# Mixture-of-experts layers on one core: each expert's combination placed ahead of the next expert's weights and gate/up product

## The reference, cut to what matters

```python
g = argmax(x @ w_group)                      # a token's group, of 4
vals, loc = top_k(elog_of_group, 2)          # two of the group's 8 experts
gates = pg * softmax(vals)
hb = silu(xb @ w_gate[e]) * (xb @ w_up[e])   # 1024 -> 512, per expert e
y[token] += gates * (hb @ w_down[e])         # 512 -> 1024
```

## Time and profile before

| | us |
|---|---|
| median of 3 runs | 1930.45 |
| lowest and highest | 1920.70, 1933.29 |
| the profiled execution, device time | 1928.58 |
| its span | 1926.7 |

### The profile page before, as it was taken

One profiled execution on the slowest core, in us unless ns is written; L12 is line 12 of the kernel. 1 busy time (PEld: TensorE's weight loads), 2 busy tenths in 40 slices (PEclk: granted clock), 3 DMA queues, 4 the chain that ended last, 5 costly groups with the idle time before them and its releaser, 6 DMA issues. The chain is left out here.

```text
span 1926.7 us, 28099 instructions
## 1 busy us (share of the span) xinstructions
PE 1617.7 (84%) x12625; PEld 1025.5 (53%) x12625; DVE 523.0 (27%) x1257; ACT 231.7 (12%) x519; POOL 75.7 (4%) x97
## 2 busy tenths in 40 slices
PE   7999768878776999957557565899999999999998
PEld 5654435444444875523233232686886446588643
DVE  5752233433134114214211111621210022521002
ACT  2311011101100001100200000120110003211000
POOL 2000100000000000000000000330000000000000
PEclk9999889988887998978787887999999999999999
DMA  9357999999998844999999999734444334143410
GB/s 343 122 231 285 377 426 424 424 424 425 426 424 343 332 193 188 421 419 410 423 407 410 426 410 425 277 138 175 169 155 151 127 113 177 42 175 133 173 44 22
DMA packets 88054, 540.04 MB, mean 280 GB/s; under 512 B 7326, under 2 KB 9438, under 8 KB 54140
## 3 DMA queue, kind: packets, MB, share of 16 engines
q1 hardware_dynamic: 86044, 531.24, 68.6%
q0 software_dynamic: 1888, 6.95, 1.0%
HBM read 531.89 MB, written 6.29 MB: 279 GB/s over the span
## 5 line engine op out<-in xcount | busy, mean ns | idle before, releaser
L725 PE MATMUL ps<-ring,work 128*32 128x256 f32 x3968 | 302.4, 467 | 223.0 <-DMA ring<-in_moe_w_up 221.5
L725 PEld LDWEIGHTS ps<-ring,work 128*32 128x32 f32 x3968 | 157.4, 130 | 355.7 <-issue 303.7
L702 PE MATMUL ps<-ring,work 128*128 128x512 f32 x768 | 331.0, 592 | 0.0
L676 PE MATMUL ps<-hT,ring 128*128 128x256 f32 (+2 forms) x1488 | 330.0, 384 | 0.0
L676 PEld LDWEIGHTS ps<-hT,ring 128*128 128x128 f32 x1488 | 283.2, 191 | 45.4 <-issue 3.3
L702 PEld LDWEIGHTS ps<-ring,work 128*128 128x128 f32 x768 | 145.7, 190 | 182.2 <-issue 181.3
L738 PE MATMUL ps<-ring,multi 128*32 128x256 f32 x1984 | 121.5, 386 | 13.7 <-ACT multi L1467 11.7
L2033 DVE TENSOR_TENSOR rowb<-rowb,ps 128x128 f32<-128x128 f32 x64 | 18.4, 288 | 386.9 <-ACT rowb L1462 386.9
L2039 DVE COPY multi<-ps 128x256 f32<-128x256 f32 x64 | 27.2, 425 | 264.7 <-PE ps L738 264.5
L738 PEld LDWEIGHTS ps<-ring,multi 128*32 128x32 f32 x1984 | 58.9, 110 | 73.8 <-issue 21.8
L1462 ACT ACTIVATE rowb<-ps 128x128 f32<-128x128 f32 x64 | 17.8, 278 | 562.4 <-PE ps L725 562.4
(11 more groups left out here) (452 smaller groups left out, 1310.8 us busy)
## 6 DMA issues: line engine op xcount, KB each, us to landing
ring<-in_moe_w_gate SPq DMA_DIRECT2D x62, 2048.0 KB, 18.8
ring<-in_moe_w_up SPq DMA_DIRECT2D x62, 2048.0 KB, 23.3
ring<-in_moe_w_down SPq DMA_DIRECT2D x62, 2048.0 KB, 22.3
ring<-in_w_ff SPq DMA_DIRECT2D x32, 2048.0 KB, 8.2
ring<-in_sc_w_in SPq DMA_DIRECT2D x6, 2048.0 KB, 17.8
ring<-in_lru_w_in SPq DMA_DIRECT2D x4, 2048.0 KB, 15.4
ring<-in_ssm_w_glu SPq DMA_DIRECT2D x4, 2048.0 KB, 18.7
ring<-in_lru_w_out SPq DMA_DIRECT2D x2, 2048.0 KB, 20.2
```

The source lines that it names most:

```text
L676: mm = pe.matmul(ps[:, bank, 0:n], w[:, k, P * c:P * c + P], hT[:, k, t0:t0 + n], start=(k == 0), stop=(k == DC - 1))
L702: mm = pe.matmul(ps[0:m, 2 + 2 * b + hf, :], left[:, kk, t0:t0 + m], w[:, k, 512 * hf:512 * hf + 512], start=(kk == 0), stop=(kk == 4 * la ...
L725: mm = pe.matmul(ps[32 * q:32 * q + 32, bank, 0:256].rearrange("p (u n) -> p u n", u=2), x[:, k, :], gu[:, k, :, 2 * P * (q // 2):2 * P * ...
```

## The change

The wait for and the issue of `weigh_in(e - 1)`, with the waits and the register load of e = 1, move from behind `gate_up` of e to a place ahead of the wait for the weights of e. Nothing is added or removed.

```diff
                     pe.wait_ge(*nth(f"xT_ready{l}", 2 * g + (1 if e == 0 else 2)))
+                    if e == 1:
+                        pe.wait_ge(*nth(f"spread_out{l}", 1))
+                        pe.wait_ge(*nth(f"rounds_known{l}", 1))
+                        rounds = pe.value_load(rounds_i[0:1, l:l + 1], min_val=1, max_val=MAX_ROUNDS)
+                    if e >= 1:
+                        weigh_in(e - 1)
                     gate_, down_ = expert_slots[l, e, "gate"], expert_slots[l, e, "down"]
...
                         gate_up(x, 4 + b, gu).then_inc(S(f"gate_up{l}"), 1)
-                    if e == 1:
-                        pe.wait_ge(*nth(f"spread_out{l}", 1))
-                        pe.wait_ge(*nth(f"rounds_known{l}", 1))
-                        rounds = pe.value_load(rounds_i[0:1, l:l + 1], min_val=1, max_val=MAX_ROUNDS)
-                    if e >= 1:
-                        weigh_in(e - 1)
                     if e in KEEP_AT:
                         keep_rows(KEEP_AT.index(e) + 1)
                     pe.wait_ge(*nth(f"hid_ready{l}", e + 1))
```

## The result

| | before | after |
|---|---|---|
| median of the runs, same chip | 1923.13 us (22 runs) | 1930.86 us (22 runs) |
| lowest and highest | 1915.24, 1935.36 | 1926.30, 1940.27 |
| the profiled execution, device time | 1928.58 | 1928.79 |
| its span | 1926.7 | 1926.8 |

Run against run the ratio is 1.003, with a 95% interval of 1.0016 to 1.0045: the change costs 3.1 to 8.7 us, some 5.8 (the two medians alone lie 7.7 us apart). That is within 1%, as forecast, but about twice the +3.1 us of the sum. That the forecast time of 1933 lies so near the 1930.86 measured is in part luck: it was built on a median of before of 1930.45 us from 3 runs, which 22 runs put at 1923.13. Two errors of opposite sign, the low sum and the high start, cancelled.

A forecast was written before the change was run, and what follows sets the result against it. Weight transfers were taken to bound both expert layers. Terms 3.7 - 0.8 + 0.7 - 1.5 + 1.0 = +3.1 us took the profiled 1928.6 to 1931.7; with the runs' median 1.9 above, 1933.6, written 1933; range 1925 to 1942 us.

The forecast's parts named there:

- The bound: Both expert layers go at the rate of the weights' transfers; TensorE counts only at late slot releases, heads and tails.
- The signs: L935's wait some 40 us, copy wait in about half the experts, idle before gate/up down 60 to 80 us, shallower dips.
- Layer 0's head: Gate/up of expert 3 ends later while transfers are dry, all of it lost: +3.7 us, between 0 and 5.
- expert 4's slot released late: Layer 0's head: expert 4's slot release, about +5 us late, might run dry too; only the upper bound of 5 us.
- Layer 1's head: Later `down` of expert 1 and gate/up of expert 3 use up the queue's cover: +0.7 us, between 0 and 2.6.
- Layer 0's tail: After the last weights come, the way from gate/up to `down` is shorter: -0.8 us.
- Layer 1's middle: `down` of the even experts comes 0.30 us sooner, five release a dry queue: -1.5 us, from 0 to 3.6 gained.
- Layer 1's tail: Expert 31's gate/up starts straight behind expert 30, so nothing covers the work put ahead of it: +1.0 us.
- Nothing at the head: Rival: something else sets the first saturated issue, the head terms vanish: -1.3 us, 1929 us; chance 0.23.
- TensorE becomes the bound in layer 0's middle: Rival: eight of experts 10 to 25 pay 1.26 us each and the queue runs dry: +10, 1943 us; chance 0.13.
- The clock pays: Rival: layer 1's even experts start gate/up at full clock, removing five dips: about -5, 1925 us; chance 0.07.
- Full price: Rival: all 62 experts pay 1.26 us because transfers never saturate: +78, 2009 us; chance 0.02.

The follow-up runs named there:

- e3: The kernel before with the combination moved ahead of gate/up only for experts 6 to 31 of both layers; 1920.49 us, ratio 0.9978 to before.
- e4: The kernel before with the combination moved ahead of gate/up only for experts 1 to 5 of both layers; 1931.96 us, ratio 1.0036 to before.
- e6: The kernel after with layer 0's combinations of experts 27, 28 and 29 issued twice, ahead of gate/up of experts 28 to 30; 1931.5 us in a single run.
- e7: The kernel before with `pick_rows` behind `down` instead of ahead of it in layer 1's even experts; 1921.25 us, ratio 0.9992 to before.
- e8: e3 with `pick_rows` behind `down` in layer 1's even experts and the old order for layer 1's expert 31; 1920.02 us, ratio 0.9981 to before.
- e1: The kernel before with the combination moved ahead of gate/up in layer 0 alone; 1927.98 us, ratio 1.0011 to before.
- e9: The kernel after with GpSimd's small loads (`load_s5`) held back until `down` of expert 5 in layer 0; 1930.18 us, ratio 1.0049 to before.
- e2: The kernel before with the combination moved ahead of gate/up in layer 1 alone; 1926.85 us, ratio 1.0004 to before.
- e12: e3 with GpSimd's small loads (`load_s5`) issued before its broadcast for the layer norm instead of behind it; 1920.26 us, ratio 0.9991 to before.
- e11: The kernel after with expert 1's `rounds_known` wait and register load put back behind its gate/up; 1925.33 us in a single run.
- e5: The kernel after with layer 0's combinations of experts 0, 1 and 2 issued twice; 1934.42 us, ratio 1.0045 to before.
- e10: e9 with layer 0's combinations of experts 0, 1 and 2 issued twice; 1936.76 us, ratio 1.0070 to before.

## Why the prediction was right, and where it was short

**The bound: right.** That the weights' transfers set both middles, and that TensorE counts at heads and tails and where its `down` releases a dry queue, is what e3, e4, e6 and e7 show. The signs came as named: the wait of L935 for L2033 is 47.4 us in 59 times (some 40 in 58 were named), the copy wait ahead of the combination shows in 28 places of 62 (25 of them without a named releaser), the idle time ahead of gate/up fell by 74 us (60 to 80), and layer 1's pairs dip less (3.6 us in all against 8.1), though the table above shows that the order isn't all of that. Layer 0's last gate/up starts later, by 6.0 us (446.5 to 452.5) where 3.7 were named.

**Layer 0's head: the right place, the wrong size.** +3.7 was worked out for the end of gate/up of expert 3; it was +5.4 in the means (35.9 to 41.25). Of this 0.4 us is the luck of which profiles had expert 0's `down` slow. Like set beside like, it is +4.9 both times: 35.92 to 40.87 with the fast `down` (before, e3, e8; e1, e6, e9) and 36.72 to 41.66 with the slow one (e2, e12; after, e4). In e7 a slow `down` was followed by a gate/up at full clock, and it stands apart at 35.0. The timeline of TensorE before the change, for the same stretch as that of after above, gives the pieces:

```profile
163.90 0.87 PE L958 MATMUL ps<-ident,work 16*128 16x16 f32 x8 [2.48 <-DVE work L2043]
...
173.75 3.81 PE L725 MATMUL ps<-work 128*32 128x256 f32 x64
...
184.68 3.85 PE L725 MATMUL ps<-ring,work 128*32 128x256 f32 x64
```

With gate/up of expert 1 from the earlier trace rows, and from after 160.59, 164.37, 174.33 and 186.30 us:

| from start to start | before | after | difference | by the sum |
|---|---|---|---|---|
| transposes L958 to gate/up 1 | 0.80 | 3.78 | +2.98 | +1.57 |
| gate/up 1 to gate/up 2 | 9.05 | 9.96 | +0.91 | 1.57 + 0.55 - 0.79 = +1.33 |
| gate/up 2 to gate/up 3 | 10.93 | 11.97 | +1.04 | 1.57 - 0.79 = +0.78 |
| all three | 20.78 | 25.71 | +4.93 | +3.7 |

The sum of these differences, +4.93, is the same figure again. The first line failed most. The first combination took 2.70 us (161.67 to 164.37), not 1.57: its two groups ran 1.72 and 1.12 us where they usually take 1.15 and 0.66, because TensorE had stood idle and ran at the low clock (the granted clock over 162 to 167 us is 0.66, between the levels of 1.2 and 2.4 GHz). And 0.42 us of idle time stands ahead of it, which e11 ties to the register load that moved there and that was costed at nothing. The sum had said that the slow time falls "partly on the combination" and changes nothing. Half of that holds: gate/up 1 took 4.35 instead of 5.15 us, which is why the second line is under its forecast. The third line is over by 0.26: the combination at 1.67 us (184.63 to 186.30) is 0.10 of it, 0.73 for the shortened way is 0.06, and 0.1 is not assigned. A gate/up straight behind `down` also began 0.18 us before that `down` had ended (173.75 against 172.00 + 1.93 = 173.93 us), and one behind a combination doesn't get that.

Behind gate/up 3 another 0.6 us were lost until gate/up 6 (+6.0 in the table, above the term's upper bound of 5). The prediction had named what may be behind this, expert 4's slot released late while the transfers are dry, and left it out of its value; no run here takes it apart. The failed step of this term is thus the price of the first combination, taken as 1.57 us from a place where TensorE ran at full clock, with its register load at nothing: it measured 2.70 us and 0.42 us of idle time.

**Layer 1's head: the margin was overrun.** +0.7 rested on 1.4 us of cover "just used up", and on gate/up 3 being late by 3.7 us. It was late by 4.3: 30.5 us in e1 and e12 and 34.8 in after, e2, e5, e9 and e10, all with expert 0's `down` at its slow pace. The timeline of TensorE after shows all three:

```profile
773.93 1.15 PE L768 MATMUL ps<-multi,tmp_a 32*128 32x256 f32 x16 [0.56 <-DVE multi L2039]
775.01 3.85 PE L725 MATMUL ps<-ring,work 128*32 128x256 f32 x64
...
782.81 1.15 PE L768 MATMUL ps<-multi,tmp_a 32*128 32x256 f32 x16 [0.60 <-issue]
783.89 3.85 PE L725 MATMUL ps<-work 128*32 128x256 f32 x64
...
794.04 3.85 PE L725 MATMUL ps<-ring,work 128*32 128x256 f32 x64
```

And its windows, the layer's first gate/up being at 763.08 us (763.83 before):

```profile
783.00:790.00 7.00, 6.29 (x85) 3.23 (x83) 1.47 (x4) 0.56 (x2) 0.00 (x0) 1.00 0.92 336
790.00:797.00 7.00, 6.99 (x106) 3.83 (x108) 1.64 (x4) 1.20 (x2) 0.98 (x2) 1.00 1.02 432
797.00:804.00 7.00, 5.58 (x61) 2.55 (x57) 1.65 (x5) 1.75 (x4) 2.45 (x2) 1.00 0.98 387
```

Two dips have opened, one behind the late `down` of expert 1 and one behind the late gate/up of expert 3; before, 781.4 to 794.3 went at 429 GB/s. At 425 GB/s they are worth (425 - 336) x 7 / 425 = 1.5 us and (425 - 387) x 7 / 425 = 0.6 us, 2.1 of the 2.8 us. The failed step is the value between the bounds: with the margin used up to within tenths, every further tenth counts whole. The +2.8 measured lies at the upper bound of 2.6 us, and slightly above it.

**Layer 0's tail: right, with a little of the luck.** -0.8 was forecast, -1.2 measured. Gate/up of expert 31 stood 2.62 us, as against 2.9 worked out, and ran 5.43 us, still at the slower pace:

```profile
601.32 5.43 PE L725 MATMUL ps<-ring,work 128*32 128x256 f32 x64 [2.62 <-issue]
```

In one kernel of the new order, e11, it ran at full clock, and there the tail was 8.9 us:

```profile
601.06 3.87 PE L725 MATMUL ps<-ring,work 128*32 128x256 f32 x64 [2.46 <-issue]
```

**Layer 1's middle: the mechanism right, the size not settled.** -1.5 forecast, -2.6 measured, or -1.5 without the profile of before; stages of one order scatter by 4 us. e7 and the table of dips show that an earlier `down` is what pays. **Layer 1's tail**: +1.0 forecast, +0.7 measured. e3 shows +0.0 there, so it may be less.

**The rivals.** "Nothing at the head" fell with e4. "TensorE becomes the bound in layer 0's middle" fell with the 425 GB/s and the 373.5 us. "The clock pays" fell too: from expert 6 on the even experts of layer 1 wait 5.6 to 10.4 us in after, and all of their gate/ups are still slow, at 5.1 to 6.6 us. One of them:

```profile
1132.81 6.40 PE L725 MATMUL ps<-ring,work 128*32 128x256 f32 x64 [9.81 <-issue]
```

"Full price" (+78 us) fell with the whole time.

The Trainium skill, "Perfetto Trace Analysis", Matmul Optimizations, wants matmuls back to back. The change raised the gaps behind gate/up from 5.5 to 47.4 us, against that rule, and where TensorE waits for weights anyway they cost nothing that the stages show (373.5 against 373.8 us); the granted clock over 218 to 596 us was 0.89 against 0.88.

## What to carry to other kernels

Where transfers set the pace, moving work on TensorE into its waits is free and gains nothing but the shorter way behind them; at a stretch's head and tail, where no wait exists, it costs its full time and the clock it meets there. So such an edit belongs behind a condition: here `e >= 6` turned a loss of 5.8 us into a gain of 4.2 (0.8 to 7.9) in the one set in which it was timed. A price read where the engine is warm doesn't hold for the first work behind an idle time: look up the clock at the place where the work will stand. When a margin is worked out to be "just used up", take the far bound. Small transfers cost less where the large ones are dry. And one profile of each kernel isn't enough for differences of a few us: set stages of several kernels beside each other, like beside like.

## What was not expected of the hardware

**A stretch of attention runs in two ways.** The rest behind layer 1 took 711 to 715 us in twelve of the fourteen profiles and 722 and 725 in e10 and e12. The windows of e3 and e12 over the same stretch:

```profile
1600.00:1700.00 100.00, 94.21 (x432) 62.58 (x431) 39.56 (x112) 24.10 (x69) 3.44 (x4) 1.00 0.30 106
```

```profile
1600.00:1700.00 100.00, 96.25 (x359) 61.59 (x358) 39.46 (x111) 21.82 (x64) 0.60 (x2) 0.86 0.29 104
```

The granted clock is 1.00 in the first and 0.86 in the second (e10 too), and TensorE gets through 432 and 359 matmuls. The group of one line shows it as time of one instruction. First e3, then e12, each as busy us, mean ns | idle before:

```profile
L1319 PE MATMUL ps<-work 64*128 64x128 f32 (+1 forms) x32 | 9.4, 375 | 0.0
```

```profile
L1319 PE MATMUL ps<-work 64*128 64x128 f32 (+1 forms) x32 | 13.6, 519 | 0.0
```

The code there is the same in all kernels. Some 10 us come and go with it, more than the change is worth, and it may be part of why the runs of one kernel spread over 20 us; only two profiles fell into it (both executions lie 7 to 8 us above the median of their kernel), so that stays an inference. It is why stages were compared and not spans.

**Small transfers take more than their bytes.** In e9 the 21 us behind GpSimd's small loads went at 308 GB/s with the DMA share at 1.01, and 18 us without them at 428 with the same share: 5.8 us lost, by the sum above. How much of this comes back depends on where they stand: e10 against e5 puts it at 3.4 us for the same dose (458.0 against 454.6), and e12 at 3.0.
